# Where VectorE takes its half of a weight split in a kernel of two transformer blocks

## The chip, the cores and the metric

The kernel runs on one core of a Trainium2 chip. The metric is the device time of one execution in microseconds (us); the kernel is run several times and the median is given. TensorE (PE in the profile) does the matrix products, VectorE (DVE) and ScalarE (ACT) the elementwise work, SyncE (SP) issues the loads of weights.

## What is computed

The reference is a model with 256 latent tokens, 256 context tokens and width 1024. Its first block has two layers; each is a feed-forward (`swiglu`), a token mixer and a second feed-forward. The mixer of the first layer is half attention and half a recurrent scan ("even mixer"); that of the second ("odd mixer") is attention with a window of 128 and a sink:

```python
        x = x + 0.5 * m_lat[:, 2] * swiglu(modulate(rms_norm(x), m_lat[:, 0], m_lat[:, 1]), ffn_in[l, 0], ffn_out[l, 0])
...
            o_lat, o_ctx = odd_mixer(h_lat, h_ctx, cos, sin, w_in, w_out, sink[o], ctx_out)
        x = x + m_lat[:, 5] * o_lat
```

Every `m_lat` is a modulation: a row of the product of `silu(c)` with a weight of 1024 x 9216 (1024 x 6144 in the second block). The second block has two layers as well. Each is a mixer with three branches, gated and added, and a feed-forward with a convolution over three tokens. The branches are `fourier_mix` (a Fourier transform over tokens and channels), differential attention, and neighbourhood attention with a bias:

```python
def fourier_mix(u):
    bsz, n, _ = u.shape
    ug = u.astype(jnp.float32).reshape(bsz, n, FN_GROUPS, FN_GROUP_DIM)
    f = jnp.fft.fft2(ug, axes=(1, 3), norm="ortho").real
```

## The kernel before, in words

**Weights.** Weights come in slabs of up to 128 x 2048 fp32 (1 MB) into a ring in SBUF, over SP's queue. A product with fp32 accuracy is built from two roundings of each factor: the weight is split into a high part `hi` (fp32r) and a rest `lo` = weight - `hi`, and three products are added: hi by hi, lo by hi, hi by lo. The activations are split in the same way (`HH`, `HL`). So a slab takes three steps ahead of PE: SP's load; ACT's copy of it to `hi` (`split` of `scalar_program`, L1424, recorded at the helper's line L1422); DVE's subtraction to `lo` (`split` of `vector_program`, L1778, recorded at L1742), which waits for the event ("hi", s). PE's first product with the slab waits for ("lo", s) (`slab_`, L990). The result buffers `WR` of a split are a pair per slot: three slots in the feed-forwards, two in the mixers (`hold["slots"]`). A ring slot is free for the next load when its `lo` is done. There are 300 such splits. The weights of modulations are used without a split (`mod_mm`: `bank<-ring,silc`).

**Order.** The whole program is one Python list, `ORDER`. Each engine runs through it and does its own part of each step, in that order, and waits for the others by semaphores; so an instruction that waits holds up all that stands behind it on its engine. The functions of a stage write its steps: `lin` a projection (steps `slab`, and `ev` for what leaves PSUM), `attention` (steps `att`: three stages of neighbouring units in one step), `fourier` (two chained products for a group of channels, with copies out of PSUM on DVE between them), `background` (modulation steps between others at a rate). `woven` merges two lists evenly. In the odd mixer the first 14 attention steps are woven with the projection of the queries, the next 14 come with modulation steps at 1.3 per attention step, then the rest of the modulations, then the activations' split and the output projection `oout` with the last attention steps.

**Placing the splits.** The loop at L944 to L963 then inserts a step ("split", s) for each slab: ahead of each `slab` step of number n it inserts the splits of the slabs n, n+1 and n+2, as far as slots and holds allow. Since slots are bound, usually the one that comes there is of a slab later than the one about to be used. Before the change one step holds both engines' halves, so DVE has its subtraction where ACT has its copy:

```python
                    if x["n"] > must or x["split_from"] > at_hold or x["last"] is not None and use[x["last"]] >= i:
                        break
                    steps.append(("split", todo.pop(0)))
            steps.append(step)
```

Other names used below: `W` is working space, `bank` PSUM, `X` the residual stream, `cst` constants, `silc` the activated conditioning, `MOD` modulations. `ev` of kind "conv" (second block's feed-forward) is an ACT copy with bias and, on DVE, two to six SCALAR_TENSOR_TENSOR for the convolution. L1754 is DVE's copy, L1751 its SCALAR_TENSOR_TENSOR, L1746 its TENSOR_SCALAR, L988 PE's product, L1209 its transpose of attention weights, L2304 SP's issue of a load.

Of the kernel before, what the change touches and what calls it, by code (L numbers as in the profile page):

```python
# [160 lines left out]
def program(nc, A, out):  # L161
    ctx = ExitStack()
    with ctx:
# [71 lines left out]
        ORDER = []  # L235
# [44 lines left out]
        def lin(name, kind, wt, groups, K, ntok, rhs=hr, ready=None, between=None, **kw):  # L280

            J = Job(name, kind, groups, K, ntok, rhs, ready, **kw)
            for g, cols in enumerate(groups):
                for k0 in range(0, K, 4):
                    kc = min(4, K - k0)
                    runs = []
                    for m, c in enumerate(cols):
                        if runs and runs[-1][0] + runs[-1][1] == c:
                            runs[-1][1] += P
                        else:  # L290
                            runs.append([c, P, m * P])
                    s = slab([(wt[k0 * P:(k0 + kc) * P, c:c + w], 0, o) for c, w, o in runs], kc, P * len(cols))
                    J.slabs.append((s, g, k0, kc))
                    last = k0 + kc == K
                    if J.ready in SHIFTS and g == 0 and grouped.setdefault(J.ready, J) is J:
                        if last:
                            first_group(J)
                        continue
                    if last and g == len(groups) - 1 and kind == "add" and ntok == NT:
                        last_slab(J, len(J.slabs) - 1, 4 * g)  # L300
                        continue
                    for m in range(len(cols)):
                        ORDER.append(("slab", J, len(J.slabs) - 1, m))
                        if last:
                            ORDER.append(("ev", J, g, m))
                            if kind == "add":
                                for h in range(ntok // 256):
                                    square(kw["norm"], 4 * g + m, h)
                    if between:
                        between()  # L310
# [171 lines left out]
        def background(gen, rate):  # L482
            tick[0] = 0.0

            def step():
                tick[0] += rate
                while tick[0] >= 1:
                    tick[0] -= 1
                    next(gen, None)
            return step  # L490
# [123 lines left out]
        def split_h(name, n, ntok, first=0):  # L614
            for k in range(first, n):
                ORDER.append(("split_h", name, k, ntok))
# [56 lines left out]
        def taken(f, *a, **k):  # L673

            n = len(ORDER)
            f(*a, **k)
            steps_ = ORDER[n:]
            del ORDER[n:]
            return steps_

        def woven(*lists):

            todo = []
            for n, x in enumerate(lists):
                groups = []
                for y in x:
                    if groups and y[0] in ("ev", "sq", "sum"):
                        groups[-1].append(y)
                    else:
                        groups.append([y])  # L690
                todo += [((i + 0.5) / len(groups), n, y) for i, y in enumerate(groups)]
            for _, _, y in sorted(todo, key=lambda z: z[:2]):
                ORDER.extend(y)
# [7 lines left out]
        def odd_mixer(mods):  # L701


            wi = A["odd_w_in"][0]
            modnorm("no", NT, 1, 3, 4)
            lin("oq0", "keep", wi, chunks(0, 4), KD, 256, ready="no", dst=lambda j: OQ[:, j, :], scale=0.125)
            lin("ok", "keep", wi, chunks(1024, 2), KD, NT, ready="no", dst=lambda j: OK[:, j, :])
            for m in range(2):
                ORDER.append(("rope", "ok", m, OK[:, m, 0:256], "rot1", "cos1", "sin1"))
            ORDER.append(("copies", "ok", [(OKD[kv][64 * e:64 * e + 64, :], OK[64 * (kv % 2):64 * (kv % 2) + 64, kv // 2, :])  # L710
                                           for kv in range(4) for e in range(2)], ("rope", "ok", 1)))
            hold["slots"] = 2
            lin_tm("ov", wi, 1280, 256, KD, "no", OV)
            ropes = lambda g: [("rope", f"oq{g}", m, OQ[:, 4 * g + m, :], "rot1", "cos1", "sin1") for m in range(4)]
            ORDER.extend(ropes(0))
            units = []
            for h, qt in pairs(16, 2):
                p0 = 64 * (h % 2)
                kv = h // 4
                u = dict(S=[(OQ[p0:p0 + 64, h // 2, qt * P:(qt + 1) * P], OKD[kv][p0:p0 + 64, P:512], P)], nk=512,  # L720
                         sink=bc[:, h:h + 1], V=[OV[:, c, 64 * kv:64 * kv + 64] for c in range(4)], skip=1,
                         out=OA[:, h // 2, qt * P:(qt + 1) * P], p0=p0,
                         ready=[(DVES, ("rope", f"oq{h // 8}", h // 2 % 4))]
                         + [(COPY[i], ("copy", "ok", 4 + i)) for i in range(4)], v_ready=(DVES, ("vt", "ov", 3)))
                if qt == 0:
                    u["bias"] = (C("wmask"), P)
                    u["lo"] = P
                else:
                    u["fill"] = C("wmask")
                units.append(u)  # L730
            att = taken(lambda: attention("oa", units, 20480))
            queries = taken(lambda: lin("oq1", "keep", wi, chunks(512, 4), KD, 256, dst=lambda j: OQ[:, 4 + j, :], scale=0.125))
            woven(queries + ropes(1), att[:14])
            step = background(mods, 1.3)
            for x in att[14:28]:
                ORDER.append(x)
                step()
            for _ in mods:
                pass
            split_h("oo", 4, 256)  # L740
            out = taken(lambda: lin("oout", "add", A["odd_w_out"][0], chunks(0, 8), KD, 256, ready="oo", mod=1, idx=5, norm="n11"))
            woven(out[:4], att[28:])
            ORDER.append(("warm",))
            split_h("oo", 8, 256, 4)
            ORDER.extend(out[4:])
            hold["slots"] = 3
# [182 lines left out]
        for s in todo:  # L929
            x = SLABS[s]  # L930
# [8 lines left out]
            if step[0] == "lora_done":  # L939
                use[LORA["s"]] = i  # L940
        befores = lambda s, kind: [x["before"] for x in SLABS[:s + 1] if x["before"] is not None and SLABS[x["before"]]["kind"] == kind]
        steps, at_hold = [], 0
        for i, step in enumerate(ORDER):
            if step[0] == "hold":  # L944
                at_hold = step[1]
            if step[0] == "mod_mm":
                assert not todo or todo[0] not in befores(step[6], "split")
            n = None
            if step[0] == "split_next":
                steps.append(("split", todo.pop(0)))  # L950
                continue
            elif step[0] in ("slab", "slab_h") or step[0] == "slab_k" and (step[4] == 1 or step[3] == 0):
                n = SLABS[step[1].slabs[step[2]][0]]["n"]
            if n is not None:
                must = n if step[0] == "slab_k" and step[4] == 0 else n + 2
                while todo:
                    x = SLABS[todo[0]]
                    if any(use[r] >= i for r in befores(todo[0], "raw")):
                        break
                    if x["n"] > must or x["split_from"] > at_hold or x["last"] is not None and use[x["last"]] >= i:  # L960
                        break
                    steps.append(("split", todo.pop(0)))
            steps.append(step)  # L963
        ORDER = steps

# [771 lines left out]
        def vector_program(e, q):  # L1737
# [37 lines left out]
                for n in ("cst", "sink", "lam"):  # L1775
                    q.wait_ge(IN[n], ("in", n))

            def split(s):  # L1778
                kc, w = SLABS[s]["kc"], SLABS[s]["w"]
                hi, lo = pair(s)  # L1780
                q.wait_ge(ACTS, ("hi", s))
                tt(lo[:, 0:kc, 0:w], slot(s)[:, 0:kc, 0:w], hi[:, 0:kc, 0:w].bitcast(F32), ALU.subtract, ("lo", s))
# [449 lines left out]
            def nc_parts(l, h, nq):  # L2232
                q.wait_ge(ACTS, ("nch", l, h))
                tt(NCl[:, h, 0:nq], NCO[:, h, 0:nq], Sh[:, h, 0:nq].bitcast(F32), ALU.subtract, ("hl", f"sc{l}", h))

            do = dict(begin=begin, inputs=inputs, inputs_rest=inputs_rest, split=split, mod_tr=mod_tr, rstd=rstd, times=times, mod_l=mod_l,
                      split_h=split_h_, y_parts=y_parts, part=part, ev=ev, ev_h=ev_h, gain=gain, bar=bar, om=om, head_sq=head_sq, head_root=head_root, head_spread=head_spread,
                      rope=rope, hsum=hsum, hroot=hroot, att=att, lora_w=lora_w, lora_t=lora_t, lora_g=lora_g, k_dir=k_dir,
                      wkv_start=wkv_start, wkv=lambda d: next(streams[d]), read_x=read_x, read_a=read_a, read_b=read_b, lam=lam,
# [168 lines left out]
```

## Time and profile before

| | us |
|---|---|
| median of 3 runs | 3925.08 (3922.23 to 3933.41) |
| the profiled execution | 3916.84 |
| its span, first to last instruction | 3915.0 |
| PE busy | 3598.5 (92% of the span) |
| DVE busy | 1895.7 (48%) |
| ACT busy | 1388.0 (35%) |

| stretch of the profiled execution (us from its start) | what runs there |
|---|---|
| 1946 to 2100 | odd mixer |
| 2440 to 2645 | second block, layer 0: differential (`da0`) and neighbourhood attention (`na0`) |
| 2664 to 2735 | its Fourier branch beside the gates' projection |
| 2913 to 3180 | its feed-forward with convolution, first half (`c0i`), with modulations in the background |
| 3327 to 3660 | layer 1: `bq1`, attention `na1`, output projection `mo1` |

A profiled execution gives the busy time of each engine, the idle time before an instruction and what ended it. Idle time matters only on the chain that ended last, which is mostly PE's here.

### The profile page before, as it was taken

What the parts mean: (1) busy time and instruction counts of PE and PEld (TensorE: products, weight loads), DVE (VectorE), ACT (ScalarE), POOL (GpSimd) and SP (SyncE); (2) the same over time, 40 slices, a digit from 0 to 9 for tenths busy, and PEclk for the clock granted to TensorE, in tenths of its full rate; (3) what the DMA queues carried; (4) which work ended last, traced back from release to release, by engine and by line L of the source; (5) the groups of instructions that cost most, each with busy time, mean ns of one, the idle gap of its engine ahead of it and who ended that gap; (6) DMA issues with size and microseconds to landing.
All of it is one profiled execution on the core that took longest, in us unless ns stands there. A gap on an engine that the chain in (4) does not pass through costs nothing.

```text
span 3915.0 us, 61954 instructions
## 1 busy us (share of the span) xinstructions
PE 3598.5 (92%) x27214; PEld 2964.7 (76%) x27214; DVE 1895.7 (48%) x3248; ACT 1388.0 (35%) x2195; POOL 60.1 (2%) x98
## 2 busy tenths in 40 slices
PE   6999999888889999999987979988999999988798
PEld 4777874777668888878756978656887778778798
DVE  2223455777754233323465444662454443564574
ACT  3213435322233233323334343442243333344453
POOL 0000000000010000000000000010000000010000
PEclk8999999999999999999998989999999999999899
DMA  5444224222243322333145542121225542233453
GB/s 188 173 164 140 76 63 145 89 99 99 88 96 96 97 92 84 119 129 123 61 162 178 185 144 76 60 60 54 87 86 180 184 159 79 97 97 108 134 178 109
DMA packets 257918, 453.93 MB, mean 116 GB/s; under 512 B 14096, under 2 KB 157584, under 8 KB 243184
## 3 DMA queue, kind: packets, MB, share of 16 engines
q1 hardware_dynamic: 253840, 441.68, 33.7%
q0 software_dynamic: 3808, 8.27, 1.3%
q8 instruction: 215, 3.52, 0.4%
q14 instruction: 55, 0.45, 0.0%
HBM read 447.24 MB, written 1.94 MB: 115 GB/s over the span
## 4 chain that ended last, share of the span: by engine, by line
PE 78%; DVE 13%; ACT 5%; DMA 2%; issue 2%; SPq 0%; POOL 0%; DVEq 0%; ACTq 0%; POOLq 0%
PE bank L988 77%; DVE WR L1742 2%; DVE W L1751 2%; DVE W L1742 2%; ACT W L1422 2%; ACT WR L1422 2%; PE bank L1209 1%; DVE W L1754 1%; DVE H L1742 1%; DVE HL L1742 1%; DVE X L1751 1%; DMA ring<-in_w_mod 1%; DMA ring<-in_w_ada 1%; DVE small L2005 1%; ACT H L1422 0%
## 5 line engine op out<-in xcount | busy, mean ns | idle before, releaser
L988 PE MATMUL bank<-HH,WR 128*128 128x512 f32 (+1 forms) x9312 | 2430.7, 348 | 94.1 <-DVE HL L1742 46.5
L988 PEld LDWEIGHTS bank<-HH,WR 128*128 128x128 f32 x9312 | 1647.8, 193 | 352.0 <-DVE HL L1742 57.9
L988 PE MATMUL bank<-HL,WR 128*128 128x512 f32 (+1 forms) x4656 | 1603.8, 344 | 0.0
L1742 DVE TENSOR_TENSOR WR<-ring,WR 128x2048 fp32r<-128x2048 f32 (+3 forms) x300 | 674.0, 2252 | 1181.1 <-ACT WR L1422 1181.1
L1422 ACT ACTIVATE WR<-ring 128x2048 fp32r<-128x2048 f32 (+3 forms) x300 | 562.5, 1881 | 1235.5 <-PE bank L988 837.5
L988 PEld LDWEIGHTS bank<-HL,WR 128*128 128x128 f32 x4656 | 898.6, 193 | 97.8 <-issue 0.7
L1422 ACT ACTIVATE W<-bank 64x256 f32<-64x256 f32 (+3 forms) x582 | 259.2, 449 | 482.1 <-PE bank L988 440.4
L988 PE MATMUL bank<-W 64*64 64x64 f32 (+5 forms) x6304 | 366.6, 252 | 59.7 <-ACT W L1422 20.4
L988 PEld LDWEIGHTS bank<-W 64*64 64x64 f32 (+3 forms) x6304 | 277.2, 144 | 152.9 <-issue 53.7
L1422 ACT ACTIVATE W<-bank,small 128x512 f32<-128x512 f32 (+2 forms) x183 | 113.0, 621 | 261.1 <-DVE small L2005 178.4
L1754 DVE COPY W<-bank 64x256 f32<-64x256 f32 (+3 forms) x352 | 135.2, 396 | 108.6 <-PE bank L988 103.9
L1742 DVE TENSOR_TENSOR W<-W,bank 128x512 f32<-128x512 f32 (+1 forms) x140 | 82.9, 597 | 180.0 <-PE bank L988 179.8
L1751 DVE SCALAR_TENSOR_TENSOR W<-bank,vec,W 128x510 f32<-128x510 f32 (+1 forms) x206 | 130.6, 634 | 79.0 <-ACT W L1422 75.2
L988 PE MATMUL bank<-ring,silc 128*32 128x512 f32 x960 | 143.3, 643 | 23.0 <-DMA ring<-in_w_mod 16.3
L988 PE MATMUL bank<-cst,W 64*64 64x64 f32 (+6 forms) x1264 | 125.6, 266 | 32.1 <-DVE W L1754 22.2
L988 PEld LDWEIGHTS bank<-cst,W 128*128 128x128 f32 (+2 forms) x1264 | 107.7, 163 | 60.1 <-DVE W L1754 24.5
L1209 PE MATMUL bank<-cst,W 128*128 128x128 f32 x432 | 77.2, 295 | 38.1 <-DVE W L1746 33.5
L1209 PEld LDWEIGHTS bank<-cst,W 128*128 128x128 f32 x432 | 48.5, 146 | 81.1 <-issue 37.4
L1422 ACT ACTIVATE W<-bank,vec 128x512 f32<-128x512 f32 (+1 forms) x136 | 83.3, 628 | 59.9 <-PE bank L988 57.9
L988 PE MATMUL bank<-WR,HH 128*128 128x512 f32 (+2 forms) x384 | 102.8, 357 | 0.0
L1422 ACT ACTIVATE H<-H,MOD 128x256 f32<-128x256 f32 x144 | 86.1, 598 | 44.4 <-DVE H L1742 44.4
L1422 ACT ACTIVATE W<-W 128x512 f32<-128x512 f32 (+2 forms) x98 | 50.1, 532 | 145.5 <-DVE W L1751 91.8
(107 smaller groups left out, 2080.2 us busy)
## 6 DMA issues: line engine op xcount, KB each, us to landing
ring<-in_ffn_in SPq DMA_DIRECT2D x176, 512.0 KB, 5.0
ring<-in_w_mod SPq DMA_DIRECT2D x72, 1024.0 KB, 5.0
ring<-in_w_in SPq DMA_DIRECT2D x52, 1024.0 KB, 5.1
ring<-in_w_ada SPq DMA_DIRECT2D x48, 1024.0 KB, 6.5
ring<-in_ffn_out SPq DMA_DIRECT2D x176, 256.0 KB, 3.6
ring<-in_w_up SPq DMA_DIRECT2D x88, 512.0 KB, 5.1
ring<-in_w_down SPq DMA_DIRECT2D x88, 256.0 KB, 3.6
ring<-in_even_w_in SPq DMA_DIRECT2D x8, 1024.0 KB, 5.1
```

Source lines behind the costliest of these rows:

```text
L988: return e.matmul(o, l, r, start=start, stop=stop, skip_group_check=True)
L1209: x = e.transpose(o[:, c * P:(c + 1) * P], a["P"][j % 3][0][:, c * P:(c + 1) * P], C("ident"))
L1422: return e.activation(o, i, f, **kw).then_inc(ACTS.sem, ACTS.mark(*events))
L1742: put(e.tensor_tensor(o, a, b, op), *events)
L1751: put(e.scalar_tensor_tensor(out=o, in0=a, scalar=s, in1=b, op0=op0, op1=op1), *events)
L1754: put(e.tensor_copy(o, a), *events)
L2005: put(e.tensor_reduce(neg, bank[:, lo:nk], AXX, ALU.max, negate=True), ("neg", name, i, j))
```

## The change

It has two parts.

1. ACT keeps its step ("split", s). DVE's half becomes a step of its own, ("rest", s). If the slab is the one about to be used, ("rest", s) stands right behind ("split", s), as before. If it is of a later slab, it is kept back, and put down just ahead of the next step that uses a slab (`slab`, `slab_h`, `slab_k` or `mod_mm`). All DVE steps between the two `slab` steps are then ahead of it. 83 of the 300 subtractions move past other DVE work; for the others nothing of DVE stands between.
2. In the odd mixer 12 attention steps instead of 14 are woven with the queries; the modulation steps begin at the 13th, at 1.4 per attention step in place of 1.3; attention steps 27 and 28 come after the last modulation. Two `split_next` steps, five steps ahead of the end of that list, place the splits of the first two slabs of `oout` between attention steps.

```diff
--- before.py
+++ after.py
@@ -730,15 +730,18 @@
                 units.append(u)
             att = taken(lambda: attention("oa", units, 20480))
             queries = taken(lambda: lin("oq1", "keep", wi, chunks(512, 4), KD, 256, dst=lambda j: OQ[:, 4 + j, :], scale=0.125))
-            woven(queries + ropes(1), att[:14])
-            step = background(mods, 1.3)
-            for x in att[14:28]:
+            woven(queries + ropes(1), att[:12])
+            step = background(mods, 1.4)
+            for x in att[12:26]:
                 ORDER.append(x)
                 step()
             for _ in mods:
                 pass
+            ORDER.extend(att[26:28])
             split_h("oo", 4, 256)
             out = taken(lambda: lin("oout", "add", A["odd_w_out"][0], chunks(0, 8), KD, 256, ready="oo", mod=1, idx=5, norm="n11"))
+            for _ in range(2):
+                ORDER.insert(len(ORDER) - 5, ("split_next",))
             woven(out[:4], att[28:])
             ORDER.append(("warm",))
             split_h("oo", 8, 256, 4)
@@ -939,14 +942,18 @@
             if step[0] == "lora_done":
                 use[LORA["s"]] = i
         befores = lambda s, kind: [x["before"] for x in SLABS[:s + 1] if x["before"] is not None and SLABS[x["before"]]["kind"] == kind]
-        steps, at_hold = [], 0
+        steps, at_hold, behind_ = [], 0, []
         for i, step in enumerate(ORDER):
+            if step[0] in ("slab", "slab_h", "slab_k", "mod_mm"):
+                steps += [("rest", s) for s in behind_]
+                behind_ = []
             if step[0] == "hold":
                 at_hold = step[1]
             if step[0] == "mod_mm":
                 assert not todo or todo[0] not in befores(step[6], "split")
             n = None
             if step[0] == "split_next":
+                behind_.append(todo[0])
                 steps.append(("split", todo.pop(0)))
                 continue
             elif step[0] in ("slab", "slab_h") or step[0] == "slab_k" and (step[4] == 1 or step[3] == 0):
@@ -959,7 +966,11 @@
                         break
                     if x["n"] > must or x["split_from"] > at_hold or x["last"] is not None and use[x["last"]] >= i:
                         break
+                    if x["n"] > n:
+                        behind_.append(todo[0])
                     steps.append(("split", todo.pop(0)))
+                    if x["n"] <= n:
+                        steps.append(("rest", steps[-1][1]))
             steps.append(step)
         ORDER = steps
 
@@ -1775,7 +1786,7 @@
                 for n in ("cst", "sink", "lam"):
                     q.wait_ge(IN[n], ("in", n))
 
-            def split(s):
+            def rest(s):
                 kc, w = SLABS[s]["kc"], SLABS[s]["w"]
                 hi, lo = pair(s)
                 q.wait_ge(ACTS, ("hi", s))
@@ -2233,7 +2244,7 @@
                 q.wait_ge(ACTS, ("nch", l, h))
                 tt(NCl[:, h, 0:nq], NCO[:, h, 0:nq], Sh[:, h, 0:nq].bitcast(F32), ALU.subtract, ("hl", f"sc{l}", h))
 
-            do = dict(begin=begin, inputs=inputs, inputs_rest=inputs_rest, split=split, mod_tr=mod_tr, rstd=rstd, times=times, mod_l=mod_l,
+            do = dict(begin=begin, inputs=inputs, inputs_rest=inputs_rest, rest=rest, mod_tr=mod_tr, rstd=rstd, times=times, mod_l=mod_l,
                       split_h=split_h_, y_parts=y_parts, part=part, ev=ev, ev_h=ev_h, gain=gain, bar=bar, om=om, head_sq=head_sq, head_root=head_root, head_spread=head_spread,
                       rope=rope, hsum=hsum, hroot=hroot, att=att, lora_w=lora_w, lora_t=lora_t, lora_g=lora_g, k_dir=k_dir,
                       wkv_start=wkv_start, wkv=lambda d: next(streams[d]), read_x=read_x, read_a=read_a, read_b=read_b, lam=lam,
```

The number of instructions of each kind on each engine is the same. PE's, ACT's and SP's order changes in the odd mixer alone. Line numbers above L964 grow by 11 (L1742 becomes L1753).

Below, each fence lists consecutive instructions of one engine in program order: line, operation, output<-inputs, size, and xN for N alike in a row.

**DVE, the Fourier branch of layer 0.** `WR<-ring,WR 128x2048` is the subtraction of a weight; `W<-bank 128x128 x2` and `W<-bank 128x256 x2` are the copies that PE's products of one `fourier` step wait for. Before:

```order
L1754 COPY W<-bank 128x128 x2
L1742 TENSOR_TENSOR WR<-ring,WR 128x2048
L1754 COPY W<-bank 128x256 x2
L1742 TENSOR_TENSOR WR<-bank,WR 128x256
L1754 COPY W<-bank 128x256 x2
L1742 TENSOR_TENSOR WR<-bank,WR 128x256
L1742 TENSOR_TENSOR WR<-ring,WR 128x2048
L1754 COPY W<-bank 128x256 x2
```

After:

```order
L1765 COPY W<-bank 128x128 x2
L1765 COPY W<-bank 128x256 x2
L1753 TENSOR_TENSOR WR<-bank,WR 128x256
L1753 TENSOR_TENSOR WR<-ring,WR 128x2048
L1765 COPY W<-bank 128x256 x2
L1753 TENSOR_TENSOR WR<-bank,WR 128x256
L1765 COPY W<-bank 128x256 x2
```

The first subtraction stood between the last attention step and the copies of the first `fourier` step; now the copies come first, and it stands behind that step.

**DVE, feed-forward with convolution of layer 0.** `W<-bank,vec,W 128x2x255` is the convolution of one group's output. Before:

```order
L1742 TENSOR_TENSOR W<-W 128x512
L1742 TENSOR_TENSOR WR<-ring,WR 128x2048 x2
L1751 SCALAR_TENSOR_TENSOR W<-bank,vec,W 128x2x255 x6
L1742 TENSOR_TENSOR W<-W 128x512
L1751 SCALAR_TENSOR_TENSOR W<-bank,vec,W 128x2x255 x2
L1742 TENSOR_TENSOR W<-W 128x512
```

After:

```order
L1753 TENSOR_TENSOR W<-W 128x512
L1753 TENSOR_TENSOR WR<-ring,WR 128x2048
L1762 SCALAR_TENSOR_TENSOR W<-bank,vec,W 128x2x255 x2
L1753 TENSOR_TENSOR WR<-ring,WR 128x2048
L1762 SCALAR_TENSOR_TENSOR W<-bank,vec,W 128x2x255 x4
L1753 TENSOR_TENSOR W<-W 128x512
```

The two subtractions stood together; now the second one has two of the convolution's instructions ahead of it, and the four others behind it.

**ACT, the end of the odd mixer's attention.** `W,small<-bank,small` is the exponential of a unit, `HH<-W 128x256 x4` the activations' split for `oout`, `WR<-ring 128x2048 x2` the copies of the first two slabs of `oout`. Before:

```order
L1422 ACTIVATE W,small<-bank,small 128x512
L1422 ACTIVATE small<-bc,small 128x1
L1422 ACTIVATE W<-bank 128x384
L1422 ACTIVATE W<-bank 128x512
L1422 ACTIVATE HH<-W 128x256 x4
L1422 ACTIVATE W,small<-bank,small 128x384
L1422 ACTIVATE small<-bc,small 128x1
L1422 ACTIVATE W<-bank 128x384
L1422 ACTIVATE WR<-ring 128x2048 x2
L1422 ACTIVATE W,small<-bank,small 128x384
```

After:

```order
L1433 ACTIVATE W,small<-bank,small 128x512
L1433 ACTIVATE small<-bc,small 128x1
L1433 ACTIVATE W<-bank 128x384
L1433 ACTIVATE WR<-ring 128x2048 x2
L1433 ACTIVATE W,small<-bank,small 128x512
L1433 ACTIVATE small<-bc,small 128x1
L1433 ACTIVATE W<-bank 128x384
L1433 ACTIVATE HH<-W 128x256 x4
L1433 ACTIVATE W,small<-bank,small 128x384
L1433 ACTIVATE small<-bc,small 128x1
```

The two weight copies stood behind the activations' split and one more unit; now they stand ahead of both, and of the unit before them.

## Rows read from the trace of the kernel before

**Rows 1.** The page's chain that ended last, by engine.

```profile
PE 78%; DVE 13%; ACT 5%; DMA 2%; issue 2%; SPq 0%; POOL 0%; DVEq 0%; ACTq 0%; POOLq 0%
```

**Rows 2.** Waits, whole run: waiter <- releaser: us in all, times, longest.

```profile
DVE WR L1742 <- ACT WR L1422: 1214.8, 267, 19.5
```

**Rows 3.** Timeline, first Fourier step: start, us, instruction, count, [idle before <-releaser].

```profile
2662.60 4.27 ACT L1422 ACTIVATE W<-W 128x512 f32<-128x512 f32 x8
...
2664.07 1.02 PE L988 MATMUL bank<-cst,W 128*128 128x256 f32 x4
...
2668.70 2.29 DVE L1742 TENSOR_TENSOR WR<-ring,WR 128x2048 fp32r<-128x2048 f32 x1 [7.12 <-ACT WR L1422]
...
2671.80 3.66 PE L988 MATMUL bank<-cst,W 128*128 128x256 f32 x8 [6.71 <-DVE W L1754]
```

**Rows 4.** Timeline, second product of the next Fourier step, which has no subtraction ahead.

```profile
2682.32 1.99 PE L988 MATMUL bank<-cst,W 128*128 128x256 f32 x8 [0.52 <-DVE W L1754]
```

**Rows 5.** Windows: us, PE, PEld, DVE, ACT, POOL busy (x), PEclk, DMA share, GB/s.

```profile
2672.00:2676.00 4.00, 4.00 (x12) 3.20 (x13) 0.08 (x1) 0.38 (x1) 0.00 (x0) 0.59 0.74 262
2680.00:2686.00 6.00, 5.48 (x26) 4.33 (x25) 1.27 (x3) 0.38 (x1) 0.00 (x0) 1.00 0.00 0
```

**Rows 6.** Timeline, last units of the neighbourhood attention, layer 0.

```profile
2640.54 2.29 DVE L1742 TENSOR_TENSOR WR<-ring,WR 128x2048 fp32r<-128x2048 f32 x1 [2.35 <-ACT WR L1422]
...
2644.77 1.63 PE L988 MATMUL bank<-W 64*128 64x256 f32 x6 [4.17 <-ACT W L1422]
```

**Rows 7.** Timeline, last units of the neighbourhood attention, layer 1.

```profile
3524.45 0.69 DVE L1742 TENSOR_TENSOR W<-W,cst 128x512 f32<-128x512 f32 x1 [3.00 <-DMA W<-skew]
...
3527.20 2.77 PE L988 MATMUL bank<-W 64*128 64x512 f32 x20 [2.20 <-ACT W L1422]
...
3533.57 1.09 PE L1209 MATMUL bank<-cst,W 128*128 128x128 f32 x4 [2.54 <-DVE W L1746]
```

**Rows 8.** Timeline of PE: a residual norm, a differential attention unit, the norm of `bq1`.

```profile
441.13 1.07 PE L988 MATMUL bank<-W,cst 128*32 128x256 f32 x16 [0.73 <-DVE X L1751]
...
2457.76 0.63 PE L1209 MATMUL bank<-cst,W 128*128 128x128 f32 x4 [1.70 <-DVE W L1751]
...
3329.72 0.71 PE L988 MATMUL bank<-cst,small 128*128 128x128 f32 x4 [3.18 <-DVE H L1742]
```

**Rows 9.** Timeline, one slab of the convolution's projection `c0i`, from issue to use.

```profile
2991.20 0.98 SPq L2304 DMA_DIRECT2D ring<-in_w_up  x2
...
2998.68 1.92 ACT L1422 ACTIVATE WR<-ring 128x2048 fp32r<-128x2048 f32 x1 [12.13 <-DMA ring<-in_w_up]
3000.50 0.76 ACT L1422 ACTIVATE W<-bank,vec 128x512 f32<-128x512 f32 x1
3000.62 2.29 DVE L1742 TENSOR_TENSOR WR<-ring,WR 128x2048 fp32r<-128x2048 f32 x1 [10.43 <-ACT WR L1422]
...
3002.83 1.53 DVE L1751 SCALAR_TENSOR_TENSOR W<-bank,vec,W 128x510 f32<-128x510 f32 x2
...
3003.65 0.50 PE L988 MATMUL bank<-HH,WR 128*128 128x512 f32 x1
```

**Rows 10.** Timeline, the last tight slab of `c0i`.

```profile
3151.33 2.29 DVE L1742 TENSOR_TENSOR WR<-ring,WR 128x2048 fp32r<-128x2048 f32 x1 [10.79 <-ACT WR L1422]
...
3153.93 0.50 PE L988 MATMUL bank<-HH,WR 128*128 128x512 f32 x1
```

**Rows 11.** Timeline, odd mixer: a held attention unit, a modulation, the first output slab.

```profile
1989.76 0.88 PE L1209 MATMUL bank<-cst,W 128*128 128x128 f32 x3 [7.07 <-DVE W L1746]
...
2036.05 1.10 PE L988 MATMUL bank<-ring,silc 128*32 128x512 f32 x8 [2.54 <-DMA ring<-in_w_ada]
...
2077.11 3.70 ACT L1422 ACTIVATE WR<-ring 128x2048 fp32r<-128x2048 f32 x2
...
2081.40 0.58 PE L988 MATMUL bank<-HH,WR 128*128 128x256 f32 x1 [6.36 <-DVE WR L1742]
```

**Rows 12.** Timeline, PE at the first slab of `mo1`.

```profile
3649.89 0.39 PE L988 MATMUL bank<-HH,WR 128*128 128x256 f32 x1 [3.64 <-DVE WR L1742]
```

## The prediction

> **What bounds the kernel.** I read the chain that ended last first [rows 1]: 78% of the span lies on PE, 13% on DVE, 5% on ACT, 2% on DMA. So most of the time is products that the change leaves alone, and it can touch only the places where PE stands still because DVE is late. Next I read the waits [rows 2]: DVE stood 1214.8 us, in 267 places, before a weight subtraction because ACT had not yet made the high part. That sum is no gain: most of it lies where DVE has nothing else to do and PE works. A piece counts only if the DVE instruction queued behind the waiting subtraction is one that PE waits for. So I went through the 83 subtractions that move, and looked in the timeline at what PE does then.
>
> **How one place pays.** The clearest is the first Fourier step [rows 3]. PE ends its first products at 2665.09 (2664.07 + 1.02). DVE should copy them out, but stands 7.12 us before the subtraction, since ACT has eight sigmoids (4.27 from 2662.60) and then the weight's copy to do; then come 2.29 us of subtraction. PE's second products start at 2671.80, after 6.71 idle, and take 3.66. In the changed order the copies are first. The next step shows what that looks like: idle 0.52, products 1.99 [rows 4].
>
> **The sum, gains.**
> - First Fourier step: 1.02 + 6.71 + 3.66 = 11.4 becomes 1.02 + 0.52 + 1.99 = 3.5: 7.9.
>   - Of this, 1.7 is the slower second product. Its stretch has a granted clock of 0.59, after the idle time, that of the other 1.00 [rows 5]: the first is mostly at 1.2 GHz, the second at 2.4 GHz.
>   - The Trainium skill ("TensorE: Matmul & The Clock Gate", Part 1: The HAM clock gate) says that an idle array falls to half clock, and comes back only some time after work resumes; by that rule, too, the 1.7 goes away with the idle time, and the trace agrees with its 0.59.
> - Three more Fourier steps have a subtraction ahead of their copies, without the sigmoids: each between 0 and what the first had in idle, 6.71 - 0.52 = 6.2. The subtraction's own 2.29 without the copy's lateness is the nearest row; PE has other products beside the first half of it. I take 1.3 each: 3.9.
> - End of `na0`: DVE idle 2.35 and subtraction 2.29 ahead of what ACT's exponential needs, PE idle 4.17 [rows 6]. At least 0, at most 4.17; I take 3.0, since the unit's own chain keeps some.
> - `na1`, two places [rows 7]. The bias copy by DMA is triggered by DVE, so it starts sooner too (DVE waits 3.00 for it): 2.2, all of PE's idle time. The second: 2.5 of 2.54. Together 4.7.
> - Two more attention units, one in `da0` with idle 1.70 [rows 8], one alike in `na0`: 3.0, bounds 0 and 3.4.
> - Two norms: the spread of `bq1` waits 3.18 [rows 8] for a DVE step behind a subtraction; 2.5 there, and at the norm ahead of the odd mixer, with a slab half as wide, 1.3. Together 3.8, bounds 0 and 5.5.
> - Six places where the evictions of a feed-forward's last slab get ahead of the subtraction; idle 0.73 in one [rows 8]. At 0.45 each 2.7, bounds 0 and 4.4.
>
> Gains 7.9 + 3.9 + 3.0 + 4.7 + 3.0 + 3.8 + 2.7 = 29.0.
>
> **The sum, losses.** DVE's subtraction now waits for DVE work that itself waits for PE.
> - Convolution, layer 0. The weight comes just in time [rows 9]: high part at 2998.68, subtraction 3000.62 to 3002.91, PE's product at 3003.65, so 0.74 is spare. DVE has been idle 10.43 before, so nothing was gained by going first except this. Now the two convolution instructions of a group (1.53) go ahead. They need ACT's copy out of PSUM, which ACT does behind the high part (3000.50 + 0.76 = 3001.26). The subtraction then starts at 3001.26 + 1.53 = 3002.79, 2.2 late: PE stalls 2.2 - 0.74 = 1.5. The last such slab has 3153.93 - (3151.33 + 2.29) = 0.31 spare and stalls 1.9 [rows 10]. Of eleven such places five are this tight; 1.6 on average makes 8.0. The others have more spare time than 2.2. Bounds: 0 (the transfers run ahead), and a rival below.
>   - The slab of 1 MB is issued at 2991.20 and its high part starts 7.5 later. The Trainium skill ("DMA: Bandwidth & Descriptors", Bandwidth) gives 6.15 us for 1 MB; were this so here, spare time would be 1.3 larger, the five stalls nearly gone, and the sum 6.5 better. I go by the row.
> - First slab of `mo1`: PE already waits 3.64 for the subtraction [rows 12]; the branch sums of DVE ahead of it add 0.9. First slab of the first feed-forward alike: 0.5.
>
> Losses 8.0 + 0.9 + 0.5 = 9.4.
>
> **The odd mixer.** Before, a subtraction holds an attention unit there: PE idle 7.07 [rows 11]. That goes, so the modulation steps, which begin two units sooner too, start and end 7 to 8 earlier; they are bound by their loads (PE idle 2.54 for DMA [rows 11]), so their own length stays. But the two units and the activations' split that are taken from beside them or from ahead of them stand behind them, in front of the output projection. Before, PE waits 6.36 there, which covers the copies of two slabs (3.70) on ACT [rows 11]. The copies now stand between units, so that order hides them, but the units' own chains have little beside them. I take the loss as 7.5, between 0 and two such waits, 12.7. So this part comes to 0, from -7 to +5.
>
> **Total.** 29.0 - 9.4 = 19.6 less. From the profiled execution's 3916.84 that is 3897.2. The median of the runs is 8.2 above that execution, so 3925.08 - 19.6 = 3905.5, and I give **3905**. A measurement of this kernel can tell about 0.3%, 11.8 us, from no change.
>
> **Rivals.**
> - *The gains in attention and norms are taken by the next wait* (a unit freed from the subtraction waits for its softmax chain instead). Of the seven gains, 3.0 + 4.7 + 3.0 + 3.8 = 14.5 go: 5.1 less, 3920. For it: the units after it have short idle times of their own, and the wait behind is always that of the last to come. Against it: the same units without a subtraction show less idle time. Chance 0.20.
> - *Nothing moves on the path.* PE works on 78% of the chain, and the amount of work is the same; the change then only relabels idle time of DVE: 0, 3925. The Trainium skill ("Perfetto Trace Analysis", Identifying the Most-Contended Engine) says to optimize the most occupied engine first, which is PE here; by that rule a change of DVE's order is worth nothing. Against it stands the 6.71 [rows 3], a wait that has the moved instruction in it. Chance 0.06.
> - *More than forecast.* The transfers run ahead in the convolution, so its 8.0 goes, and the odd mixer gives 8: 35.6 less, 3889. For it: PE's other stalls there give the load queue time. Against it: the weights land just in time in a stretch in which modulation weights share the queue. Chance 0.20.
> - *Slower: the late subtraction delays the loads.* A ring slot is free when its subtraction is done, so a subtraction 2.25 late delays the load that goes into it, and where loads bound the stretch, PE pays twice: once for the subtraction, once for the transfer. At all eleven places of the convolution that is 11 x 4.5 = 49.5 in place of 8.0: 41.5 more, hence 3905.5 + 41.5 = 3947. It decides the sign when the load queue has no slack: from 3.6 a place (39.4 in all) the kernel is slower by over 11.8. Against it: only five places are tight, and the two subtractions of a place release their slots 2.25 apart. Chance 0.06.
>
> **How the numbers follow.** My forecast has 0.48. Its terms' bounds make about 3897 to 3913. The range reaches to the rival above, 3889, a little beyond it to 3887, and to 3921, past the first rival; outside are the slower case, the case of no change, and a part of the larger gain, 0.19 in all. Faster by over 0.3% (below 3913.3): 0.48 less a little, and 0.20, and a bit of the first rival: 0.68. Within 0.3%: 0.26. Slower: 0.06.
>
> **What would show it.** Right: PE's idle time before the second product of the first Fourier step is about 0.5 and the granted clock there 1.0; the waits of DVE's subtraction for ACT fall well below 1214.8; PE waits 1.4 to 1.9 for `WR` at five slabs of the convolution; the modulation stretch starts about 8 sooner, and the time to the output projection is about as before. Wrong: stalls at all eleven slabs, or loads that are issued later than before; attention units with the same idle time and another releaser; or a wait before the output projection that is gone or twice as long.

## The result and the profile after

| | before | changed |
|---|---|---|
| median, us | 3924.18 (4 runs, 3922.23 to 3933.41) | 3888.04 (4 runs, 3886.03 to 3892.14) |
| profiled execution, us | 3916.84 | 3892.14 |
| its span | 3915.0 | 3890.3 |
| granted clock, mean | 0.965 | 0.969 |

The ratio is 0.9905, with a 95% interval of 0.9887 to 0.9922: about 37 us less. I had forecast 20 less. The time lies at the edge of the range given, and the size is wrong by almost a factor of two. The two profiled executions alone differ by 24.7, so the time has to be looked for in two places: in the terms of the sum, and in what one profiled execution stands for.

The page of the changed kernel, the chain that ended last and the waits (waiter <- releaser: us in all, times, longest), to be set beside [rows 1, 2]:

```profile
PE 79%; DVE 12%; ACT 4%; DMA 3%; issue 2%; SPq 0%; DVEq 0%; ACTq 0%; POOLq 0%
```

```profile
DVE WR L1753 <- ACT WR L1433: 915.7, 206, 16.9
```

DVE's wait before a subtraction fell by 299 us, in 61 places fewer; the chain lost one point each of DVE and ACT. These 299 us less of DVE's waiting came with some 37 us less of time; as the prediction said of such a sum, most of it hid nothing.

The timeline at the first Fourier step of the changed kernel, to be set beside [rows 3]:

```profile
2657.76 1.02 PE L999 MATMUL bank<-cst,W 128*128 128x256 f32 x4
2658.39 0.86 DVE L1765 COPY W<-bank 128x256 f32<-128x256 f32 x2 [3.12 <-PE bank L999]
2659.39 1.97 PE L999 MATMUL bank<-cst,W 128*128 128x256 f32 x8 [0.61 <-DVE W L1765]
2660.47 1.90 ACT L1433 ACTIVATE WR<-ring 128x2048 fp32r<-128x2048 f32 x1
2663.01 2.28 DVE L1753 TENSOR_TENSOR WR<-ring,WR 128x2048 fp32r<-128x2048 f32 x1
```

The copies now start when PE's products are there, the idle time is 0.61 in place of 6.71, and the second products take 1.97 in place of 3.66. The windows (us; PE, PEld, DVE, ACT, POOL busy; PEclk; DMA share; GB/s) show the clock at full:

```profile
2650.00:2664.00 14.00, 13.39 (x71) 10.24 (x70) 2.77 (x6) 9.47 (x15) 0.00 (x0) 1.00 0.01 1
```

One slab of the convolution in the changed kernel, the same one as in [rows 9]:

```profile
2980.05 1.92 ACT L1433 ACTIVATE WR<-ring 128x2048 fp32r<-128x2048 f32 x1 [14.16 <-DMA ring<-in_w_up]
2981.87 0.76 ACT L1433 ACTIVATE W<-bank,vec 128x512 f32<-128x512 f32 x1
2982.66 1.53 DVE L1762 SCALAR_TENSOR_TENSOR W<-bank,vec,W 128x510 f32<-128x510 f32 x2 [13.38 <-ACT W L1433]
2984.11 2.28 DVE L1753 TENSOR_TENSOR WR<-ring,WR 128x2048 fp32r<-128x2048 f32 x1
2986.45 0.50 PE L999 MATMUL bank<-HH,WR 128*128 128x512 f32 x1 [1.41 <-DVE WR L1753]
```

DVE is idle for 13.38. The high part is there at 2981.97 (2980.05 + 1.92), and still DVE begins the subtraction only at 2984.11: 2.1 late, and PE stands 1.41. That is the loss as forecast (1.5). The Trainium skill ("DMA: Bandwidth & Descriptors", Bandwidth) has 6.15 us for 1 MB, but as the busy span of the transfer engines alone, which it says lies below the time from end to end. So it can't be set against the 7.5 from issue to use, as the prediction did, and the stalls came as the row said.

The odd mixer: the first modulation product after the queries, and PE ahead of the output projection, to be set beside [rows 11]:

```profile
1989.45 0.52 PE L1220 MATMUL bank<-cst,W 128*128 128x128 f32 x3 [3.00 <-DVE W L1757]
...
2021.61 1.94 PE L999 MATMUL bank<-ring,silc 128*32 128x512 f32 x8
...
2078.65 0.88 PE L999 MATMUL bank<-W 128*64 128x128 f32 x12 [4.11 <-ACT W L1433]
...
2084.66 0.58 PE L999 MATMUL bank<-HH,WR 128*128 128x256 f32 x1 [4.33 <-DVE WR L1753]
```

The 7.07 of idle time is 3.00 now, and the modulations begin 4.3 sooner (2025.87 in before's trace). This execution was 3.6 late when it entered the odd mixer, so within the mixer they begin 7.9 sooner, as forecast (7 to 8). Behind them PE waits 1.89 and 4.11 in attention units and 4.33 for the slab, where it waited 6.36 once: 4.0 more. The units themselves now stand there with little beside them. The output projection begins at 2084.66 in place of 2081.40, which within the mixer is 0.4 sooner: gain and loss cancel, as forecast.

### The profile page after: what moved, and what is told of

Same layout as the page of the kernel before. It is cut to its first block, busy times and chain, and to the rows that moved or that the text cites. A ratio compares the mean times of both kernels' runs of the same rounds, so it can differ in the third digit from the quotient of the medians.

```text
span 3890.3 us, 61958 instructions
## 1 busy us (share of the span) xinstructions
PE 3593.7 (92%) x27214; PEld 2962.0 (76%) x27214; DVE 1894.1 (49%) x3248; ACT 1387.4 (36%) x2195; POOL 60.1 (2%) x98
## 4 chain that ended last, share of the span: by engine, by line
PE 79%; DVE 12%; ACT 4%; DMA 3%; issue 2%; SPq 0%; DVEq 0%; ACTq 0%; POOLq 0%
PE bank L999 78%; DVE W L1762 3%; DVE W L1753 2%; DVE WR L1753 2%; ACT W L1433 2%; ACT WR L1433 1%; PE bank L1220 1%; DMA ring<-in_w_up 1%; DVE W L1765 1%; DVE H L1753 1%; DMA ring<-in_w_ada 1%; DVE HL L1753 1%; DMA ring<-in_w_mod 1%; DVE X L1762 1%; DVE W L1768 0%
## 5 line engine op out<-in xcount | busy, mean ns | idle before, releaser
L1753 DVE TENSOR_TENSOR WR<-ring,WR 128x2048 fp32r<-128x2048 f32 (+3 forms) x300 | 673.6, 2250 | 882.5 <-ACT WR L1433 882.0
L1753 DVE TENSOR_TENSOR W<-W,bank 128x512 f32<-128x512 f32 (+1 forms) x140 | 83.0, 598 | 203.9 <-PE bank L999 203.7
L999 PE MATMUL bank<-cst,W 64*64 64x64 f32 (+6 forms) x1264 | 123.4, 264 | 21.2 <-DVE W L1765 12.7
L2016 DVE TENSOR_REDUCE small<-bank 128x1 f32<-128x512 f32 (+1 forms) x128 | 73.0, 587 | 74.6 <-PE bank L999 73.4
```

What stands on the lines that cost most here:

```text
L999: return e.matmul(o, l, r, start=start, stop=stop, skip_group_check=True)
L1753: put(e.tensor_tensor(o, a, b, op), *events)
L2016: put(e.tensor_reduce(neg, bank[:, lo:nk], AXX, ALU.max, negate=True), ("neg", name, i, j))
```

## The experiments

All kernels but the changed one and the two copies of before are built from the change; each edit is given against it. Each set has its own runs of the kernel before, and "less" goes by the ratio to them.

**The two kernels again.**

> The kernel before, unchanged, for a second profiled execution. Theory A (the two profiled executions are not alike in stretches that the change leaves alone; before's was a short one, after's a long one): time against before 0, profiled span 3920 or above, with 5 to 8 us more than the first profile between 600 and 1900. Rival B (the first profile is typical): profiled span within 3 us of 3915.

Measured: 3922.68 against 3922.72; profiled span 3914.1. The expectation of a span of 3920 fell, and Rival B holds as worded: the span is within 3 of 3915. But the profiled execution was the shortest of its twelve (3915.85, the others to 3947.47).

> The changed kernel, for a second profiled execution and a tighter ratio. Theory A: 36 us faster than before, profiled span 3884 to 3887, and the stretch from 950 to 1110, where the first profile lost 5.4 us, loses nothing. Rival B (the change itself costs there): the same 5 us are lost again.

Measured: 3889.61, ratio 0.9916 (0.9900 to 0.9933), 33 us less; profiled span 3888.1. The span is 1 above the range expected. From 950 to 1110 this profile lost nearly 5 us again, so Theory A falls as worded. But it isn't the change that costs there: before's own second profile lost 4 in that stretch, two later kernels with no subtraction moved there (`e5_fourier_only`, `e10_att_only`) lost 5, and two with the kept-back subtraction (`e6_all_but_fourier`, `e7_no_conv`) lost nothing.

**The two parts of the change apart.**

```diff
-            woven(queries + ropes(1), att[:12])
-            step = background(mods, 1.4)
-            for x in att[12:26]:
+            woven(queries + ropes(1), att[:14])
+            step = background(mods, 1.3)
+            for x in att[14:28]:
...
-            ORDER.extend(att[26:28])
...
-            for _ in range(2):
-                ORDER.insert(len(ORDER) - 5, ("split_next",))
```

> The kept-back subtraction alone, the odd mixer's order as before. By my sum this is the whole effect: 36 us faster than before, equal to the changed kernel within 4. Rival (the odd mixer's order gives the part that my sum lacked): about 20 faster, the rest missing.

Measured: 3885.20, ratio 0.9902 (0.9884 to 0.9920), 38 less. The second part alone leaves each subtraction right behind its copy:

```diff
             if step[0] == "split_next":
-                behind_.append(todo[0])
                 steps.append(("split", todo.pop(0)))
+                steps.append(("rest", steps[-1][1]))
                 continue
...
-                    if x["n"] > n:
-                        behind_.append(todo[0])
                     steps.append(("split", todo.pop(0)))
-                    if x["n"] <= n:
-                        steps.append(("rest", steps[-1][1]))
+                    steps.append(("rest", steps[-1][1]))
```

> The odd mixer's order alone, each subtraction right behind its copy. My sum: 0, from -7 to +5. Rival (the odd mixer gives what my sum lacked): 12 to 17 us faster than before.

Measured: 3922.24, ratio 0.9996 (0.9985 to 1.0007), which is from 6 less to 3 more. So the kept-back subtraction is the whole effect as far as can be measured, and the odd mixer's new order gives nothing. Its profile has a span 11.6 longer than before's first, though. The windows of that stretch show why, here, then in the first profile of before:

```profile
620.00:645.00 25.00, 25.00 (x95) 9.90 (x96) 8.02 (x21) 9.51 (x21) 0.00 (x0) 0.59 0.36 124
```

```profile
620.00:645.00 25.00, 24.44 (x150) 9.95 (x152) 13.91 (x36) 12.95 (x30) 0.00 (x0) 1.00 0.73 252
```

PE does 95 matmuls instead of 150 in 25 us, busy all the time, at a granted clock of 0.59 instead of 1.00, so mostly at 1.2 GHz. Neither kernel's program differs there: this is between executions.

**Where the gain lies.** The subtraction is kept back in some places only, with the odd mixer's order as before (that part of the edit isn't shown again):

```diff
-                    if x["n"] > n:
+                    late = x["n"] > n and step[1].name in ("g010", "g011")
+                    if late:
                         behind_.append(todo[0])
                     steps.append(("split", todo.pop(0)))
-                    if x["n"] <= n:
+                    if not late:
```

This edit doesn't touch the branch of `split_next`. So in this kernel and in every other that keeps back "only" somewhere, three more subtractions stay kept back: one ahead of the first feed-forward, one at the norm ahead of the odd mixer, one at the norm of `bq1`. In the traces of these kernels the two norms give about 1.5 and 2.3, 3.8 together. And `g010` and `g011` are layer 0's gates alone, not those of both layers, as the expectation says; layer 1's Fourier steps are untouched by the change in any case.

> The subtraction is kept back only where the next slab is one of the gates' beside the Fourier steps (both layers); elsewhere and in the odd mixer as before. In the profiled executions this stretch gave 12.8 us. Theory A (the 8 to 10 us by which the timed runs of before lie above its profile come from the clock, which falls after the 6.7 us of idle time there): median 20 us faster than before. Rival B (they are spread over other stretches): 13 faster.

Measured: 3907.37 against 3918.94, ratio 0.9967 (0.9952 to 0.9982), 13 less, with an interval of 7 to 19. Theory A falls. In the profile the stage with the Fourier steps is 12.8 shorter.

The complement, `not in`:

> The complement: kept back everywhere but there, odd mixer as before. In the profiled executions the rest gives 27.2 - 12.8 = 14.4. Theory A: 14 faster. Rival B: 22 faster.

Measured: 3898.93, ratio 0.9938 (0.9919 to 0.9956), 24 less (17 to 31): Rival B. The part that my sum lacked is in this half. 13 + 24 = 37 looks like an exact sum, but both kernels hold the 3.8 of the two norms, and the intervals are 6 and 7 us wide on each side.

With `step[1].kind != "conv"`:

> Kept back everywhere but in the convolution's projections, odd mixer as before. The five stalls of 1.4 to 1.6 (7.5 in all in the profile of the changed kernel) go: 7.5 faster than the kept-back subtraction alone, 44 faster than before, profiled span about 3879. Rival (PE would wait for the loads anyway, so the time is only paid elsewhere): equal to the kept-back subtraction alone.

Measured: 3877.40, ratio 0.9888 (0.9867 to 0.9908), 44 less, as expected, and 6 less than the kept-back subtraction alone, where 7.5 was expected; the intervals hold both. Its span, 3871.1, is 8 below the expected one. With `step[1].kind == "conv"`:

> Kept back only in the convolution's projections. My sum: five stalls of about 1.5, 7.5 slower than before, of which five places show in the profile. Rival (late subtractions delay the loads, each place pays twice): 25 or more slower, and loads issued later.

Measured: 3922.09 against 3918.94, ratio 1.0000 (0.9984 to 1.0015), from 6 less to 6 more. The times don't show 7.5 more. They shouldn't: the 3.8 of the two norms, which this kernel gains too, leaves 3.7. The loss itself is seen in the profile. PE's products of the convolution's projection (group, count, busy, mean ns, idle before and what ended it) in before, in this kernel and in the one without the delay there:

```profile
L988 PE MATMUL bank<-HH,WR 128*128 128x512 f32 (+1 forms) x728 | 219.0, 380 | 0.1
```

```profile
L997 PE MATMUL bank<-HH,WR 128*128 128x512 f32 (+1 forms) x728 | 219.0, 380 | 7.5 <-DVE WR L1751 7.3
```

```profile
L997 PE MATMUL bank<-HH,WR 128*128 128x512 f32 (+1 forms) x727 | 218.6, 380 | 0.6 <-DVE WR L1751 0.6
```

The 7.3 are five places of 1.2 to 2.0. Nothing is paid twice: the rival with delayed loads falls. (Ten places of this stage have a moved subtraction, not eleven as in the prediction; the other five don't stall.)

Next, beside all of that kernel but the convolution, layer 1's Fourier steps, which the change missed: they stand two products behind the copy, not one.

```diff
-            if step[0] in ("slab", "slab_h", "slab_k", "mod_mm"):
+            if step[0] in ("slab", "slab_h", "slab_k", "mod_mm") and not (step[0] == "slab" and step[1].name in ("g110", "g111") and step[3] == 1):
                 steps += [("rest", s) for s in behind_]
```

> As the kept-back subtraction everywhere but in the convolution, odd mixer as before; in addition, beside layer 1's Fourier steps the subtraction is kept back one product more, so that it comes behind the Fourier step's copies. Theory (the gain per place is the idle time in front of the copies): the four idle times there, 4.2, 1.3, 1.6 and 1.3, fall to about 0.5 each, 6 us less than without this edit: 50 faster than before. Rival (the subtraction, later now, is waited for by the next slab's first product, two products further on): no gain, and PE waits for WR there.

Measured: 3870.00 (3868.26 to 3872.87), ratio 0.9862 (0.9841 to 0.9883), 54 less: the fastest here. First of layer 1's Fourier steps, its second products, in the kernel with the kept-back subtraction only and in this one:

```profile
3529.03 3.78 PE L996 MATMUL bank<-cst,W 128*128 128x256 f32 x8 [4.18 <-DVE W L1762]
```

```profile
3508.87 2.00 PE L997 MATMUL bank<-cst,W 128*128 128x256 f32 x8 [0.52 <-DVE W L1763]
```

Again the idle time and the slow second product go together, 3.7 + 1.8. All four idle times are 0.52 now, and no product of the gates waits for `WR`, so the rival falls; the whole stage became 6.7 shorter, where 6 was expected.

Kept back beside attention only (`step[1].name` one of `oq`, `cq`, `ck`, `cv`, `g00`, `g10`, `u`):

> Kept back only where the steps of attention are woven with projections (odd mixer's queries, both layers of the second block), odd mixer's order as before. Theory A (each place has its own gain and they add): in the profile 7.0 less between 2355 and 2645, 8.5 less between 3352 and 3565, in the odd mixer about 0, nothing elsewhere: 15.5 faster in the median. Rival B (the units' gains are larger in timed executions than in profiled ones, since without them the clock falls more often): 22 or more faster, and a narrower spread of the times than before's.

Measured: 3908.01, ratio 0.9951 (0.9928 to 0.9974), 19 less, with an interval of 10 to 28. In the profile the attention of layer 0 is 6.8 shorter and that of layer 1 8.0, near the 7.0 and 8.5 of Theory A; with the 3.8 of the two norms, which Theory A left out, its 15.5 becomes 19.3. The times spread from 3895.44 to 3918.78, not much less than before's, so nothing here speaks for Rival B, though the interval doesn't exclude its 22. Its profile is long in the very stretch seen above:

```profile
620.00:645.00 25.00, 25.00 (x93) 9.61 (x92) 8.24 (x21) 7.95 (x17) 0.00 (x0) 0.56 0.34 123
```

> The kernel before, a third profiled execution. Theory A (executions differ in the scan with modulations, 618 to 1166, and in the odd mixer, and nowhere else by over 2.5 us): every other stage within 2.5 us of the first profile. Rival B: it differs also in the stages where the change gains.

Measured: 3922.10, span 3920.3.

> The same, a fourth one; by Theory A at least one of the four lies 4 us or more above the first in the scan.

Measured: 3922.82, span 3920.9. Theory A holds: outside of the scan and the odd mixer no stage of the four is over 2.5 off, and in the scan the second is 4.0 longer and the fourth 7.3.

## Why the prediction was wrong in size

With four profiles of before and several of kernels that keep the subtraction back, the stages can be compared as means. I take the time of the first product of each stage in each trace, and form the stage's length less that in the first profile of before. "Kept back" is the mean of the changed kernel's two profiles and of the one without the odd mixer's edit (for the odd mixer of the first two).

| stage (us in the first profile) | four of before | kept back | difference | forecast |
|---|---|---|---|---|
| to 619: first feed-forward, even attention | -0.6 (-1.7 to 0.3) | -3.1 | -2.5 | 0 |
| 619 to 1166: scan with modulations | 2.8 (-0.1 to 7.3) | 4.3 (2.5 to 7.4) | 1.5 | 0 |
| 1166 to 1943: two feed-forwards | 0.0 | -0.8 | -0.8 | -0.9 |
| 1943 to 2153: odd mixer | 0.3 (-2.4 to 4.0) | 0.7 (-0.5 to 1.8) | 0.4 | -1.3 |
| 2153 to 2355: feed-forward | -0.6 | -1.5 | -0.9 | -0.4 |
| 2355 to 2770: attention, Fourier, layer 0 | -0.3 | -21.2 | -20.9 | -17.8 |
| 2770 to 2932 | 0.4 | -1.0 | -1.4 | 0 |
| 2932 to 3187: convolution | 0.9 | 8.7 (7.6 to 10.2) | 7.8 | 8.0 |
| 3187 to 3352: its output, norm of `bq1` | 1.1 | -1.3 | -2.4 | -3.0 |
| 3352 to 3565: attention, layer 1 | -0.5 | -8.5 | -8.0 | -4.7 |
| 3565 to 3732: branches, `mo1` | -0.2 | -2.8 | -2.6 | 0.9 |
| from 3732 | -0.2 | -0.9 | -0.7 | -0.4 |
| sum | | | -30.5 | -19.6 |

**Right.** The mechanism of most terms: the Fourier step with idle time and clock together; the convolution's loss, 7.8 measured and 8.0 forecast, at five places and for the reason given; the odd mixer at nothing, with its gain ahead of the modulations and its loss behind them; the idle times of the attention units; the two norms, 3.8. The rival "nothing moves on the path" falls with the 6.71. The Trainium skill ("Perfetto Trace Analysis", Identifying the Most-Contended Engine) only names the engine to optimize first. The prediction took from this that a change of DVE's order is worth nothing, which doesn't follow: by that order PE's own idle time became shorter here, and the run by 0.95%. "The gains are taken by the next wait" fell too: each stage of attention in the second block gave all of its term and more. At one place it did happen in part: ahead of `bq1` the wait of 3.18 is gone, and a new one of 1.64 stands a few products on. "More than forecast" had nearly the right time (3889) for reasons that didn't come true: neither did the convolution's stalls go, nor did the odd mixer give 8. That it was near is luck.

**Wrong, the first part: terms too small.** 11 us of the sum, and over half of them are the clock. The step that failed: attention places, and three of the four Fourier steps, were priced by PE's idle time alone ("2.2, all of PE's idle time", "I take 1.3 each"), while products at the lower clock behind the idle time were counted at the first Fourier step only (1.7). With the means of the table above, a stage's change can be parted into PE's idle time and PE's busy time, for the same products in the same number (the parts are rounded by themselves):

| stage | idle | forecast | busy | forecast |
|---|---|---|---|---|
| 2355 to 2770: attention, Fourier, layer 0 | -16.3 | -16.1 | -4.5 | -1.7 |
| 3352 to 3565: attention, layer 1 | -5.0 | -4.7 | -3.0 | 0 |

The idle times were forecast well. The busy time lacked 5.8. One place shows how: the same 16 products of PE behind the idle time of 2.54 [rows 7], in the first profile of before and in that of the changed kernel:

```profile
3533.50:3537.00 3.50, 3.44 (x16) 3.38 (x16) 2.36 (x7) 1.89 (x6) 0.00 (x0) 0.50 0.75 283
```

```profile
3513.80:3516.00 2.20, 2.06 (x16) 1.88 (x16) 2.13 (x6) 1.61 (x6) 0.00 (x0) 1.00 0.00 0
```

At a granted clock of 0.50 (1.2 GHz) they take 3.44, at 1.00 (2.4 GHz) 2.06. The end of `na0` is alike: behind its idle time of 4.17 before has a clock of 0.51 from 2644.7 to 2648, the changed kernel 1.00 in the same products. How much of this an execution pays varies: among the four profiles of before the busy time of layer 1's attention differs by up to 1.5, and 3.0 is the difference of the means.
- In layer 1 there was also a place that I hadn't counted: one unit ahead of the two, PE was idle 0.89 at 3518.97 and isn't any more. A new wait of 0.51 behind the two takes part of it back.
- `mo1`, "the branch sums of DVE ahead of it add 0.9": no loss, as PE waits 3.38 there in place of 3.64. At its second slab it waits 2.79, 3.03 and 1.57 in the three kept-back profiles, 4.48 and 3.65 in the first and third of before. The first feed-forward, "alike: 0.5": no loss seen either. Both losses were put in without a row that shows a product held up by the sums; why `mo1` gained instead wasn't traced further. The 2.5 up to 619 can't be put down to the change: in the kernel with the odd mixer's order alone no subtraction is moved there, and its stretch is 2.7 shorter.

**Wrong, the second part: one execution taken for the kernel.** "The median of the runs is 8.2 above that execution" was carried over as a constant. It is none. The first profile of before had the shortest scan of the four but for 0.1, at 0 where another had 7.3, and its execution, 3916.84, was below all its timed ones. The changed kernel's first profile lost 7.4 in the scan, and its execution, 3892.14, was the longest of its four. So the pair shows 24.7 where the medians show 36. The means by stage give 30.5, of which the scan is +1.5, within what it varies by itself; without it 32.0. The timed ratios give 37 (33 in the second set, 38 without the odd mixer's edit). What lies between 32 and 38 stays open: it is within the intervals (0.9887 to 0.9933 is 26 to 44), and no run tells whether the change makes low clock in the scan rarer. Over all fourteen profiles the scan took 1.0 more than in the first one on average in the six that keep the subtraction back nearly everywhere (-3.9 to 7.4), and 5.9 in the eight others (-0.1 to 20.5); that is a hint, and the ranges overlap. Only one moved subtraction stands in that stage, at 1152, near its end.

The range had a fault of its own. "Its terms' bounds make about 3897 to 3913" isn't the sum of the bounds given: the lowest and highest values of the terms, added up, go from about 2 slower to 54 faster.

## What to carry to other kernels

When one step belongs to two engines, place it on each by itself: the second engine's half need not stand where the first's does, and everything behind a wait at the head of its queue pays. Keep it back only as far as there is spare time ahead of its consumer: where the operand comes just in time (here 0.3 to 0.7 us before use), go first; where other work of that engine feeds the bound engine, go last. And take more than one profiled execution before a sum of small terms, note which stages vary, and at each idle time of PE that goes read the granted clock of the products behind it: where it is low, they get shorter too.

## What the runs showed that I had not expected

Most of the difference between executions of one kernel sits in the scan with its modulations, and some in the odd mixer. Against the first profile of before, the scan's stage took -3.9 to 8.5 more in all profiles but one, and 20.5 in that one. In the two longest the granted clock of 620 to 645 is 0.59 and 0.56, with PE busy for 25.00 of 25 us, and 1.00 in the first profile of before with PE busy for 24.44. So a stretch of many short products, almost without idle time in it, ran at little over half the clock for 25 us, in kernels whose program isn't changed there. In all fourteen profiles PE stands 2.36 or 2.37 just before, ending between 613 and 618. In seven of them the clock falls about there: in five it is soon back, in these two it stays at half for 24 and 27 us. In the other seven it doesn't fall. The Trainium skill ("TensorE: Matmul & The Clock Gate", Part 1: The HAM clock gate) ties the half clock to an idle array. The traces agree as to the fall at the Fourier steps and, where it comes, here. They don't agree as to the 24 and 27 us at half clock with PE busy by the profile; here the measurement decides.

The changed kernel is one of the five. Its stretch from 600 to 620 shows a clock of 0.91 with 2.4 us without PE work, as does that of the kernel with the odd mixer's order alone (0.91, PE busy 17.64 in both), yet the changed one had 1.00 afterwards:

```profile
600.00:620.00 20.00, 17.64 (x91) 10.62 (x91) 9.00 (x22) 6.97 (x17) 0.56 (x1) 0.91 0.15 42
620.00:645.00 25.00, 24.43 (x152) 9.74 (x150) 14.80 (x39) 13.52 (x31) 0.00 (x0) 1.00 0.68 241
```

Which of the two ways an execution goes there isn't told by what stands ahead of it in these traces.
